# Head of block 1: first quarter of the input ahead of the first weights, parameters in two loads, squares added by VectorE, S5 tables behind the first norm

## The reference

```
xn   = rms_norm(h, ln1_g)                    # h * rsqrt(mean(h*h) + 1e-6) * g
proj = xn @ w_in                             # split into u_s5, q, k, v, gate_logits
step = exp(log_step); mag = exp(lr * step)   # per state: 32 groups x 64 states
abar = mag * (cos(li * step) + i sin(li * step))
h    = associative_scan(h_t = abar * h_(t-1) + bbar @ u_t)     # the S5 branch
y_s5 = (gelu(Re(c @ h) + d * u)) @ w_glu ... @ w_s5_branch
y_attn = sliding_window_attention(q, k, v, norms, biases, sinks) @ w_attn_branch
h = h + (g_s5 * y_s5 + g_attn * y_attn) @ w_out
h = h + peer_mixer(rms_norm(h, ln2_g), ...)  # 16384 experts
```

## Time and profile before

| | |
|---|---|
| median of 3 runs | 1654.24 us (1653.69 to 1656.99) |
| the profiled execution | 1653.12 us |
| its span, first to last instruction | 1651.3 us |
| TensorE busy | 1580.5 us, 96% of the span |
| VectorE, ScalarE, GpSimd busy | 871.0, 913.9, 1197.1 us |
| TensorE idle before its first matmul | 7.74 us |

### The profile page before, as it was taken

How to read it: one execution, slowest core, us unless ns; L and a number is a source line. 1 busy time by engine, 2 the same in 40 slices (tenths; PEclk the granted TensorE clock), 3 DMA queues, 4 the chain that set the end, 5 groups by cost and what they waited for, 6 DMA issues and landing times.

```text
span 1651.3 us, 35141 instructions
## 1 busy us (share of the span) xinstructions
PE 1580.5 (96%) x14340; PEld 1515.4 (92%) x14340; DVE 871.0 (53%) x1790; ACT 913.9 (55%) x1549; POOL 1197.1 (72%) x500
## 2 busy tenths in 40 slices
PE   7998999999999999999999999898999998899997
PEld 7986989999999999999999999677999996789997
DVE  6987445993366667777511134956220079552101
ACT  6776665445444445555566656465553356656533
POOL 5653777998887787787888887215888861268885
PEclk9999999999999999999999999999999999999999
DMA  7442555566555555555666656513566664146663
GB/s 248 140 141 65 192 179 169 190 197 189 189 177 172 177 180 169 177 178 171 198 195 196 194 181 178 179 39 128 180 196 196 194 180 141 52 144 195 197 193 115
DMA packets 89631, 279.57 MB, mean 169 GB/s; under 512 B 19200, under 2 KB 19968, under 8 KB 89216
## 3 DMA queue, kind: packets, MB, share of 16 engines
q1 hardware_dynamic: 89472, 277.34, 53.5%
HBM read 276.25 MB, written 1.05 MB: 168 GB/s over the span
## 4 chain that ended last, share of the span: by engine, by line
PE 79%; DVE 8%; ACT 4%; issue 4%; POOL 3%; DMA 0%; DVEq 0%; SPq 0%; POOLq 0%; ACTq 0%
PE ps L2747 21%; PE ps L2091 12%; PE ps L2419 10%; PE ps L2730 7%; PE ps L2731 7%; PE ps L2735 7%; PE ps L538 6%; POOL wl L199 2%; ACT wh L184 1%; DVE attention L1880 1%; PE ps L2716 1%; PE ps L2217 1%; PE ps L2718 1%; ACT attention L1662 1%; DVE small L1885 1%
## 5 line engine op out<-in xcount | busy, mean ns | idle before, releaser
L199 POOL TENSOR_TENSOR wl<-slots,wh 128x1024 fp32r<-128x1024 f32 x236 | 573.0, 2432 | 315.2 <-ACT wh L184 304.1
L2528 POOL TENSOR_TENSOR wl<-slots,wh 128x1024 fp32r<-128x1024 f32 x256 | 619.2, 2422 | 123.9 <-ACT wh L2466 121.8
L2466 ACT ACTIVATE wh<-slots 128x1024 fp32r<-128x1024 f32 x256 | 271.8, 1062 | 345.2 <-issue 219.5
L184 ACT ACTIVATE wh<-slots 128x1024 fp32r<-128x1024 f32 x236 | 249.9, 1061 | 239.0 <-PE ps L2419 98.9
L2730 PE MATMUL ps<-xh,wh 128*128 128x256 f32 x1024 | 242.1, 279 | 0.0
L2747 PE MATMUL ps<-xh,wh 128*128 128x256 f32 x1016 | 239.8, 279 | 1.2 <-ACT wh L2466 1.2
L2731 PE MATMUL ps<-xl,wh 128*128 128x256 f32 x1024 | 239.0, 277 | 0.0
L2747 PE MATMUL ps<-xl,wh 128*128 128x256 f32 x1016 | 237.1, 277 | 0.0
L2730 PEld LDWEIGHTS ps<-xh,wh 128*128 128x128 f32 x1024 | 192.4, 188 | 0.1
L2731 PEld LDWEIGHTS ps<-xl,wh 128*128 128x128 f32 x1024 | 192.5, 188 | 0.0
L2747 PEld LDWEIGHTS ps<-xh,wh 128*128 128x128 f32 x1016 | 190.9, 188 | 1.4 <-ACT wh L2466 1.4
(11 more groups left out here) (385 smaller groups left out, 2994.6 us busy)
## 6 DMA issues: line engine op xcount, KB each, us to landing
slots<-w SPq DMA_DIRECT2D x254, 512.0 KB, 4.1
slots<-wu SPq DMA_DIRECT2D x128, 512.0 KB, 3.6
slots<-wv SPq DMA_DIRECT2D x128, 512.0 KB, 4.1
arena<-bias SPq DMA_DIRECT2D x1, 2048.0 KB, 8.4
attention<-w SPq DMA_DIRECT2D x6, 256.0 KB, 4.7
h<-xT SPq DMA_DIRECT2D x4, 256.0 KB, 6.5
arena<-keys SPq DMA_DIRECT2D x1, 1024.0 KB, 8.7
yT<-y_out SPq DMA_DIRECT2D x2, 512.0 KB, 2.7
```

The costliest lines, as they stand in the source:

```text
L184: act.activation(self.hi[:, n % 2, :], self.slots[:, u % SLOTS, :], ACT.Copy).then_inc(self.rounded, 1)
L199: pool.tensor_tensor(self.lo[:, n % 2, :], self.slots[:, self.order[n] % SLOTS, :], self.hi[:, n % 2, :].bitcast(F32), ALU.subtract).then_ ...
L2466: act.activation(whv[:, r % 2, :], slots_v[:, r % SLOTS, :], ACT.Copy).then_inc(w_hi, 1)
L2528: pool.tensor_tensor(wlv[:, r % 2, :], slots_v[:, r % SLOTS, :], whv[:, r % 2, :].bitcast(F32), ALU.subtract).then_inc(w_lo, 1)
```

## The change

It has six parts, all in the functions of block 1.

1. SP: the parameters are loaded in two pieces. The first 110 columns (all but `cs5`) come first; the other 512 columns come after the fourth unit, with a semaphore of their own, for which DVE waits just before it reads `cs5`. The first quarter of the input is issued ahead of the first unit.
2. ACT: the first two chunks of the input are converted before the first unit is rounded, not after.
3. ACT squares the input in two halves, and DVE adds the four squares of each half (`add_squares`, L391), so that TensorE's sum is over 2 chunks, not 8. TensorE takes it between the two halves of `("u", 1)`, not ahead of them; the banks' order changes with it.
4. ACT: the root for the norm and `e64` come before the sines of the angles, `table(0)` and `turns_of(1)`.
5. ACT: the places of the roundings between these move. Between the absolute value of the first table and its sines stands the rounding of the seventh unit.
6. DVE: `angles(0)` comes after the reciprocal and `uT`, not before.

```
         def first_sync(sp):
-            sp.dma_start(p1[:, :], par1).then_inc(loaded_p, 16)
-            unit(0)
-            for quarter in range(4):
-                cols = slice(quarter * 2 * T, (quarter + 1) * 2 * T)
-                sp.dma_start(h[:, cols], xT[:, cols]).then_inc(loaded_x[quarter], 16)
+            sp.dma_start(p1[:, 0:narrow], par1[:, 0:narrow]).then_inc(loaded_p, 16)
+            quarter_of_x(0)
+            unit(0)
+            for quarter in range(1, 4):
+                quarter_of_x(quarter)
             unit(1)
             sp.dma_start(cst[:, :], consts[:, 0:NEARLY]).then_inc(loaded_c, 16)
             unit(2)
             unit(3)
+            sp.dma_start(p1[:, narrow:NPAR1], par1[:, narrow:NPAR1]).then_inc(loaded_cs, 16)
         def first_act(act):
-            ring.round(act, 1)
             for c in range(DC):
+                if c == 2:
+                    ring.round(act, 1)
                 if c % 2 == 0:
                     act.wait_ge(loaded_x[c // 2], 16)
                 act.activation(xhT[:, c, :], hT[:, c, :], ACT.Identity, scale=par("ln1")[:, c:c + 1])
             ring.round(act, 1)
+            for half in range(2):
+                act.activation(sq[:, 4 * half:4 * half + 4, :], hT[:, 4 * half:4 * half + 4, :],
+                               ACT.Square).then_inc(s_sq, 1)
             act.wait_ge(s_dve, 2)
             link(act.activation(s5[:, MAG], s5[:, LS], ACT.Exp))
-            act.activation(sq, hT, ACT.Square).then_inc(s_sq, 1)
+            ring.round(act, 2)
+            b = banks.take(act, "ms")
+            banks.give(root_of_mean(act, b, D, std[:, 0:T]), "ms")
+            banks.wait_drained(act, "ms")
+            link(act.activation(e64, std[:, 0:T], ACT.Square, scale=float(np.sqrt(64.0 * EPS))))
+            ring.round(act, 1)
             act.wait_ge(s_dve, 9)
             link(act.activation(s5[:, SIN], s5[:, TAU], ACT.Sin, scale=TURN))
             link(act.activation(s5[:, COS], s5[:, TAUC], ACT.Sin, scale=TURN))
             ring.round(act, 1)
             act.wait_ge(s_zero, 2)
-            table(0)
+            table(0, (0,))
+            ring.round(act, 1)
+            table(0, (1, 2))
+            act.wait_ge(loaded_c, 16)
             turns_of(1)
-            ring.round(act, 1)
-            b = banks.take(act, "ms")
-            banks.give(root_of_mean(act, b, D, std[:, 0:T]), "ms")
-            banks.wait_drained(act, "ms")
-            link(act.activation(e64, std[:, 0:T], ACT.Square, scale=float(np.sqrt(64.0 * EPS))))
-            ring.round(act, 3)
             b = banks.take(act, "turn").rearrange("p (k n) -> p k n", n=P)
         def first_dve(dve):
-            dve.wait_ge(loaded_c, 16)
-            angles(0)
+            for half in range(2):
+                dve.wait_ge(s_sq, half + 1)
+                add_squares(dve, sq[:, 4 * half:4 * half + 4, :], half, s_pre0)
             banks.wait_drained(dve, "ms")
             dve.reciprocal(rst[:, 0:T], std[:, 0:T]).then_inc(s_r1, 1)
             ...
+            dve.wait_ge(loaded_c, 16)
+            angles(0)
             angles(1)
             ...
+            dve.wait_ge(loaded_cs, 16)
             cs = par("cs5").rearrange("p (s k c) -> p k s c", k=2, c=16)
         def first_pe(pe):
-            pe.wait_ge(loaded_c, 16)
-            sum_squares(pe, "ms", sq, DC, (s_sq, 1))
-            pair_product(pe, ("u", 1), xhT, xlT)
+            def first_sum():
+                pe.wait_ge(loaded_c, 16)
+                sum_squares(pe, "ms", added, 2, (s_pre0, 2))
+
+            pair_product(pe, ("u", 1), xhT, xlT, between=first_sum)
```

More of the change, by code:

```diff
@@ L481, in build @@
         loaded_x = [sem(f"loaded_x{quarter}") for quarter in range(4)]
-        loaded_p, loaded_c, loaded_b, loaded_s = (
-            sem(n) for n in ("loaded_par", "loaded_consts", "loaded_bias", "loaded_s5"))
+        loaded_p, loaded_c, loaded_b, loaded_s, loaded_cs = (
+            sem(n) for n in ("loaded_par", "loaded_consts", "loaded_bias", "loaded_s5", "loaded_outputs"))
+        s_pre0 = sem("squares_added0")
         s_zero, s_dve, s_a3, s_xhi, s_xlo, s_sq, s_r1 = (
@@ L497, in build @@
         four, three, upper = (0, 1, 2, 3), (5, 6, 7), (4, 5, 6, 7)
-        banks.plan([("u", 0), "ms", ("u", 1), "k", "turn", ("q", 0), ("q", 1), ("q", 2), ("q", 3), "v", "qs"]
+        banks.plan([("u", 0), ("u", 1), "ms", "k", "turn", ("q", 0), ("q", 1), ("q", 2), ("q", 3), "v", "qs"]
                    + [("g", i) for i in range(8)] + [("t", 0), ("t", 1)], three)
@@ L524, in over, with pair_product @@
             return ap.rearrange("p (o t) -> p o t", o=1).broadcast_to([P, n, T])
-        def pair_product(pe, job, hi, lo, ready_hi=None, ready_lo=None):
+        def pair_product(pe, job, hi, lo, ready_hi=None, ready_lo=None, between=None):
             bank = banks.open(pe, job)
@@ L543, in pair_product @@
                 for j in range(2):
+                    if j and between:
+                        between()
                     w = by_chunk(ring.high(pe))
@@ L581, in unit, with quarter_of_x @@
                 ring.load(sp, w1[u, :, :])
-            sp.dma_start(p1[:, :], par1).then_inc(loaded_p, 16)
-            unit(0)
-            for quarter in range(4):
+            narrow = PAR1["cs5"][0]
+            def quarter_of_x(quarter):
                 cols = slice(quarter * 2 * T, (quarter + 1) * 2 * T)
                 sp.dma_start(h[:, cols], xT[:, cols]).then_inc(loaded_x[quarter], 16)
+            sp.dma_start(p1[:, 0:narrow], par1[:, 0:narrow]).then_inc(loaded_p, 16)
[3 more added lines that the diff above has]
+                quarter_of_x(quarter)
             unit(1)
@@ L949, in first_dve @@
             b = banks.take(dve, "ks")
-            dve.wait_ge(s_a3, 6)
+            dve.wait_ge(s_a3, 3)
             dve.tensor_tensor(two(b[:, :]), two(b[:, :]), over(e64, 2), ALU.add).then_inc(s_ke, 1)
@@ L967, in first_dve @@
             link(dve.reciprocal(col(RDN), col(DN)))
-            dve.wait_ge(s_a3, 4)
+            dve.wait_ge(s_a3, 5)
             link(dve.tensor_tensor(col(NR), col(MAG), col(COS), ALU.mult))
```

## The result

| | before | after |
|---|---|---|
| median of 20 runs each, in turn | 1655.85 us | 1658.97 us |
| lowest and highest | 1652.40, 1660.57 | 1655.94, 1663.93 |
| ratio after to before | | 1.0020 (95%: 1.0011 to 1.0029) |
| profiled execution | 1653.12 | 1661.78 |

The account below looks back on a forecast made before the run. TensorE (busy 96%) and VectorE hold each other; TensorE's 3.9 us lead becomes a 0.8 lag, then waits 2.5 more, VectorE 3.2 late: both 3.2 later, 1654.24 + 3.2 = 1657.4 us. Range 1654.3 to 1660.1.

Parts of the forecast that it names:

- Start: First loads and input conversions: last conversions done at about 10.3 us instead of 11.0, TensorE gains 0.7 us.
- Squares: Sum of squares for the norm: TensorE's 4 rows instead of 16 gain 2.4 us; VectorE leads by 4.2 us.
- The cover: Slack between VectorE's sums of squares ending (16.6 us) and TensorE being ready for them (19.4): 2.8 us.
- the holds: GpSimd subtractions and VectorE angle steps exclude each other; the first three steps take 6.2 us, with 3.15 when GpSimd is quiet.
- Tables behind the norm: First angles and ScalarE's queue behind the norm: rotation starts at 37.7 to 37.8 instead of 34.60, VectorE 3.2 us later.
- TensorE behind it: TensorE after s5_inputs(0): waits for rounded units turn its lead into a lag; it ends 3.2 us late like VectorE.
- Lead: TensorE's lead over the kernel before at s5_inputs(0): 3.9 us, at 29.5.
- The wait behind the keys' root: TensorE waits 2.5 us for a unit rounded behind the root of the keys' sums, which comes 3.2 later.
- At nothing: Second parameter load, third change of ScalarE's function table and the later fifth unit were taken to cost nothing.
- faster: Rival: TensorE keeps its 3.9 us lead, needing VectorE through 1.6 us earlier; 1650.3 us, chance 0.08.
- The holds don't come: Rival: angles(0) meets GpSimd idle, 3.15 us not 6.2, rotation at 34.7; +0.1 us, 1654.3, chance 0.14.
- The rule that the prediction put beside its rows: Two-SBUF-input or two-port VectorE instructions and SBUF-reading GpSimd ones block each other; reductions never do: angle steps pay, sums don't.

Follow-up runs that it names:

- e5: Kernel before with only the new loads and the new order of the first conversions; rotation at 34.50 us, ratio to before 0.9996.
- e10: Changed kernel with the loads and the first rounding as before; rotation at 39.48 us, ratio to before 1.0025.
- e12: Kernel before, unchanged, timed and profiled against itself; rotation at 35.29 us, ratio 0.9992.
- e1: Changed kernel with the first tables' steps on VectorE and ScalarE ahead of the first norm again; rotation at 36.73 us, ratio to before 1.0011.
- e4: Changed kernel with GpSimd's subtractions from the fifth unit on waiting for the first angles; rotation at 38.03 us, ratio to before 1.0016.
- e8: e7 with the two first angle steps left on VectorE put between its sums and its reciprocal; rotation at 32.00 us, ratio to before 0.9977.
- e9: e8 with the second first-group angle step behind the norm's products and the seventh rounding behind the first table; rotation at 31.09 us, ratio to before 0.9979.
- e11: e8 once more, on the chip of e9; rotation at 32.63 us, ratio to before 0.9980.
- e7: Changed kernel with ScalarE making both groups' time-angle products and the seventh rounding before the absolute value, the first group's taken from VectorE; ratio to before 0.9994.
- e6: Changed kernel with TensorE summing all eight chunks of squares, no sums on VectorE; rotation at 40.47 us, ratio to before 1.0032.
- e3: Changed kernel with only the seventh unit's rounding moved ahead of ScalarE's absolute value; rotation at 38.77 us, ratio to before 1.0029.

## Why the prediction was right

The forecast was 3.2 us and 3.1 came, and the path was the one foretold. That the two differ by only 0.1 is luck: the interval of the measurement is 1.5 us to each side, and some terms below were off in opposite directions. What carries the claim is the path in the profile, 3.43 us at the rotation and 3.40 at the group of 58.40. Step by step:

- *Start.* Foretold: conversions over at 10.3, 0.7 us gained. Measured 10.02, since all six last conversions start at 7.51 and not 8.5. What of it reaches TensorE is mis-sized or at least unknown: 0.1 us (e5) to 1.45 (e10), with a scatter of 0.7 in the same place (e12).
- *Squares.* Sum of 4 rows foretold at 19.4, 0.9 us: 19.61, 1.03. The root ended at 21.15, not 20.7 (0.2 of that from the sum's start, the rest from the two releases). The cover was sized wrongly: 2.8 us foretold, 1.3 measured, as the sums ended at 18.32 and not 16.6. The six last low parts of the input took 6.36 us, where before all eight took 3.83: GpSimd's subtractions, started at 7.63 and 11.26, now lie on them; one of the six took 2.62 us, where the median is 0.48. They read two SBUF inputs, as two of the three angle steps do, and I had weighed the holds for the angle steps and the sums only. It cost nothing, since 1.3 us were left; e1 shows the price with the cover gone.
- *Tables behind the norm.* Angle steps foretold 23.8 to 30.0, 6.2 us: 24.17 to 30.31, 6.06 without the gaps, of which 2.9 are holds (e4). ScalarE's queue foretold 30.1 to 35.8: 30.40 to 36.13. Rotation foretold at 37.7 to 37.8: 38.03.
- *TensorE behind it.* Lead foretold 3.9: 3.71. Four waits foretold 4.7 in sum, lag 0.8: TensorE lost 3.71 + 0.83 = 4.54 to the keys' sums. The brackets give only 1.28 + 0.33 + 0.96 + 1.10 = 3.67 of it: they count from the modelled end of the matmul before, and such an end lies some 0.15 us behind the next start when nothing waits, so each wait is longer than its bracket. The wait behind the keys' root foretold 2.5: from 0.83 to 3.40 behind (L574 at 61.80; before at 58.40), 2.57, with brackets of 1.65 and 0.34.
- *At nothing.* The second load, the third change of ScalarE's table (46.40 to 47.68, with the root waiting until 50.72) and the fifth unit cost nothing that shows.

Of the rivals, "faster" needed VectorE 1.6 us earlier. e8, e9 and e11 confirm the mechanism: with the queue of ScalarE freed of its wait, the same start and the same squares give 0.2% less than before (in e7, which went half the way, the time is not told from before). "The holds don't come" was wrong in its condition. Its price stays open: e4 takes the holds away only by making the low parts later, and then the rotation is as late. The rule that the prediction put beside its rows, the Trainium skill (SBUF — State Buffer, "Who interferes with whom"), held in the rows read here: steps with two SBUF inputs or in a two-port mode went from 3.14 to 6.06 us with GpSimd beside them, and the two sums, reductions, kept 3.99 us for two while a subtraction ran from 16.11 (the first, with GpSimd idle for most of it, 2.01 us, the second 2.07).

What the prediction did not see is that its parts can't be added. Taking the rotation: the move of the tables costs 5.97 us with TensorE summing the squares (e6 against e5) and 1.30 with VectorE summing them (after against e1). The sums on VectorE cost 2.23 us with the tables ahead (e1 against e5) and save 2.44 with the tables behind (after against e6). The pairs with e5 also hold the new place of TensorE's sum and the squaring in halves, which no run took apart, and each of these numbers carries the start's scatter of up to 0.7 us; the gap between 5.97 and 1.30 is well beyond it. I walked one of the two ways from e5 to the changed kernel, and its sum was right.

## What to carry to other kernels

When a step moves behind another, look at the whole queue of the engine that waits for it, and put in front of the wait what doesn't depend on it: here two groups of products (e7), with the first angle steps moved into VectorE's own gap (e8), which turned a loss of 0.2% into a gain of as much. Two engines that hand work to and fro (angles, table, products, angles) pay each queue's place twice. And measure a head by a landmark behind which the order is the same, less the scatter of its own start: that told 0.2 us, where 20 runs told 1.5. It holds only as far as the clock is the same in both profiles.

## What the hardware showed that I had not expected

Behind waits of TensorE its granted clock fell to half (1.2 of 2.4 GHz) for one stretch of 3.4 us or two: from 23.4 in e1 behind a wait of 3.65 us, from 35.6 in e3 within one of 4.12, and in the changed kernel behind this wait (TensorE, then the stretch and the one after it):

```profile
140.92 0.30 PE L423 MATMUL ps<-cst,arena 128*128 128x128 f32 x1 [4.07 <-DVE arena L890]
```

```profile
141.90:145.30 3.40, 3.40 (x18) 2.16 (x16) 2.80 (x5) 1.82 (x5) 0.00 (x0) 0.50 0.00 0
145.30:148.70 3.40, 2.98 (x28) 1.95 (x24) 1.84 (x3) 2.19 (x6) 0.00 (x0) 1.00 0.00 0
```

But it isn't the length of the wait alone: a wait of 1.97 us at 118.60 was followed by such a stretch in the profile of before, and the same wait at 121.89 was not in that of after. Nor does it take a wait at all. The longest half-clock stretch of the first 120 us, in before and after alike, begins within a group of 32 matmuls of two columns each, in front of which no wait is recorded (before; then the clock):

```profile
64.67 4.07 PE L1269 MATMUL ps<-cst,arena 128*128 128x2 f32 x32
```

```profile
67.70:74.50 6.80, 6.80 (x40) 6.56 (x40) 6.55 (x16) 1.85 (x5) 0.83 (x1) 0.50 0.43 145
```

In the after profile it is as long (70.2 to 77.0, clock 0.50). In e12, which is the kernel before, it was half as long (0.51 from 68.8 to 72.2, then 0.99), and the same work, from TensorE's second group of L571 to the first of L1184, took 33.21 us instead of 34.52. So e12, 0.69 us behind at the rotation, is 0.63 ahead at 118.60. The 3.29 us at L1204 agree with the forecast also because both profiles have the long stretch.

So the places and lengths of these stretches differ from one execution to the next. Most of what the two profiled executions differ by beyond the head is of this kind: the start of the same VectorE instruction was 3.3 us later at 117 us, 5.3 at 300 to 900 and 8.7 at 1100, with more half-clock stretches on the side of after (162.4, 1056.7 and 1080.6 us, against one at 1002.9 before). It is a reason why single profiles are a bad measure of 3 us. It is argued from the places of these stretches, and no run took them away; but the times go with the clock as well. Of the changed kernel's 20 executions the four with a mean granted clock of 0.995 have a median of 1656.2 us, the three with 0.992 one of 1662.0; of the 29 of the kernel before that were timed with e9 to e11, the nine with 0.995 have 1654.1 and the three with 0.992 have 1659.9.
